# Five engines' strands interleaved by tables of knots in place of beat formulas

## Chip, cores and metric

One Trainium2 chip, one of its cores. The metric is device microseconds from start to end of one execution; lower is better. The kernel before took 2063.88 us, the median of 3 runs (2056.12 to 2064.72).

## What is computed

Two transformer blocks follow each other on 256 tokens of width 1024, all in float32. Cut to what matters:

```python
def first_block(x, mem, ...):
    x = x + token_mixer(rmsnorm(x, g_mix), ...)        # stick-breaking attention + gated delta rule
    x = x + memory_cross_attention(rmsnorm(x, g_cross), rmsnorm(mem, g_mem), ...)
    x = x + peer(rmsnorm(x, g_peer), w_pq, peer_subkeys, peer_u, peer_v)
    return rmsnorm(x, g_final)

def peer(xn, w_pq, subkeys, peer_u, peer_v):           # 8 heads, 16384 experts, top 16 each
    q = (xt @ w_pq).reshape(T, 8, 2, 128)
    s = jnp.einsum('thpd,hpnd->thpn', q, subkeys)
    top_s, top_i = lax.top_k(s, 16)
    # 256 pair sums per head, the best 16 of them, softmax gates
    act = gelu(einsum('thkd,td->thk', peer_u[expert], x)) * gate
    return einsum('thk,thkd->td', act, peer_v[expert])

def second_block(x, ...):                              # gated linear attention + spatial gating, then peer_2
```

So each block has a front of projections and attention, and then a "peer" layer in which every token picks 128 of 16384 experts.

## The kernel before, in words

The 256 tokens are two tiles of 128 (t = 0 and 1). Each of the two layers' peer parts (l = 1 and 2) handles its tiles in different ways. For tile 0 the rows of `peer_u` are gathered: 128 indirect DMAs of 128 rows by GpSimd (`rows`, through `gather`, L2328), each followed by a dot product with the normed tile. Two of three dots are done by VectorE (`experts`, L2103), every third by GpSimd (`dots`, L2351) with the sum taken by ScalarE (`experts` of the scalar program, through `act`, L1177). For tile 1 all 128 chunks of the transposed table stream through four buffers `ut_sb` (SyncE, `dense`, L592) and TensorE multiplies each (`dense`, L1013). One-hot products (`gates`, L1032) spread the gate weights. Then `values` multiplies the gates with all 128 chunks of `peer_v` (L1051, L1053, L1065), while tile 0's first 640 columns come from gathered rows (`lows`, L2328).

Before the gathers come `queries` (L977), `scores` (L992) and `select` on VectorE: per pair of heads j = 0 to 3 a strand of some 42 small pieces (`max`, `match_replace`, `max_index`, one-hot sums), of which the last writes the gather's indices `idx_sb` (L1685, signal "ix").

**What sets the order.** Each engine has one instruction stream, which it works off in order. The stream is written by a program of generators ("strands"), one for each task. A strand yields a beat (a number) before each of its pieces, and `in_turn` always advances the strand with the least beat, ties by its place in the list; a beat under the strand's last one counts as that one. The beat is a sort key and nothing else: no instruction waits for it. Waits are on semaphores and stand inside the pieces. In the kernel before the beats come from formulas: `P1(n) = 20 + 6.8 n` for the first projection, `gdn_beat`, `sel_beat`, `dense_beat`, `T_VAL` and others.

```python
        first = min(heads, key=lambda x: (x[0], x[1]))
        beat = next(first[2], None)
        ...
            first[0] = max(beat, first[0])
```

Places that the prediction touches:

- VectorE, front: `splits` (the low half of each weight chunk, `tt` at L1679, out `w_lo`) stands at `P1(n) - 4`, the pieces of `conv` of projection n at `P1(n) + 7` to `P1(n) + 9.1`. TensorE's projections (`proj`, L631 to L633) wait for `w_lo`.
- VectorE, `select(1, 0)`: pieces 35 to 40 of j = 0 (`sel_beat + 6.5 + 0.5 n`, from L1682 to L1685) stand among the cross-attention pieces of `mixer1(1)`, of which one waits for a score bank (L1956).
- ScalarE, `queries(1, 0)` piece 3 (copies a query bank to `sw_sb`, which `scores(1, 0)` piece 3 on TensorE reads) has beat 398, behind `experts(1)` pieces 16 and 19, which wait for GpSimd's dots.
- TensorE: `scores(1, 0)` piece 3 stands behind `dense(1)` pieces 0 and 1.
- Layer 2: `select(2, 0)` on VectorE stands among `mixer2(1)`, whose pieces wait for TensorE's L874; on TensorE `peer_norm(2, 0)` (transposes, L638) stands ahead of `mixer2(1)` (L874, L891).
- SyncE: the first four loads of `dense(2)` have beat 1250 and so stand behind most of the weights of `mixer2(1)` and `queries(2, ...)`, the last of which wait for TensorE.

Of the kernel before, what the change touches and what calls it, by code (L numbers as in the profile page):

```python
# [64 lines left out]


# [95 lines left out]
T_VAL = {1: (768, 2.1), 2: (1713, 2.4)}  # L162
# [65 lines left out]
def build(nc, a):  # L228
    with ExitStack() as ctx:
# [168 lines left out]
        def sync_program(e):  # L398
# [218 lines left out]
            in_turn(first(), weights(), weights2(), rows(), subkeys(), dense(1), values(1), dense(2), values(2), store())  # L617
# [3 lines left out]
        def tensor_program(e):  # L621
# [58 lines left out]
            def norm_mem():  # L680
                for t in range(2):
                    yield from transposed(ring_m, ("mem",), t, MN[:, t, :], ((28, 29), (41, 42))[t], "xs", norm_v)
# [470 lines left out]
            def sgu(t):  # L1153
# [6 lines left out]
                for g in range(4):  # L1160
# [4 lines left out]
            in_turn(norm_x(), norm_mem(), proj(), gdn(0), stick(0), row("peer", 1, ring_c, ROW, 124), mixer1(0), memory(), stick(1),  # L1165
                    peer_norm(1, 0), gdn(1), queries(1, 0), scores(1, 0), mixer1(1), experts(1, 0), peer_norm(1, 1), queries(1, 1), scores(1, 1),
                    dense(1), experts(1, 1), gates(1, 1), gates(1, 0), values(1), row("final", 1, ring_c, ROW, T_VAL[1][0] + 20),
                    row("ln", 1, ring_c, LNR, 970), norm_2(), keys(), proj2(), gla(0), sgu(0), gla(1), sgu(1),
                    row("peer", 2, ring_c, ROW, 1161), mixer2(0), mixer2(1), peer_norm(2, 0), queries(2, 0), scores(2, 0), experts(2, 0),
                    peer_norm(2, 1), queries(2, 1), scores(2, 1), dense(2), experts(2, 1), gates(2, 1), gates(2, 0), values(2),  # L1170
                    row("final", 2, ring_c, ROW, T_VAL[2][0] + 20))


        def scalar_program(e):
# [488 lines left out]
            def sgu(t):  # L1663
# [4 lines left out]
            in_turn(norm_x(), splits(), norm_mem(), proj(), silus(), betas(), gdn(0), stick(0), row("peer", 1, ROW, 126), mixer1(0), memory_hi(),  # L1668
                    memory(), stick(1), gdn(1), peer_norm(1, 0), mixer1(1), queries(1, 0), softmax(1, 0), experts(1), peer_norm(1, 1),
                    queries(1, 1), softmax(1, 1), dense(1), gates(1, 1), gates(1, 0), values(1), row("final", 1, ROW, T_VAL[1][0] + 21),  # L1670
                    row("ln", 1, LNR, 971), final(1, 0), final(1, 1), norm_2(), keys(), proj2(), gla(0), sgu(0), gla(1), sgu(1),
                    row("peer", 2, ROW, 1162), peer_norm(2, 0), queries(2, 0), softmax(2, 0), experts(2), peer_norm(2, 1),
                    queries(2, 1), softmax(2, 1), dense(2), gates(2, 1), gates(2, 0), values(2), row("final", 2, ROW, T_VAL[2][0] + 21),
                    final(2, 0), final(2, 1))

        def vector_program(e):
# [573 lines left out]
            def sgu(t):  # L2250
# [27 lines left out]
                else:  # L2278
# [3 lines left out]
            in_turn(norm_x(0), norm_x(1), splits(), norm_mem(), conv(), betas(), gdn(0), stick(0), mixer1(0), memory_lo(), stick(1), gdn(1), peer_norm(1, 0),  # L2282
                    experts(1), weights(1), select(1, 0), mixer1(1), peer_norm(1, 1), select(1, 1), gates(1, 1), dense(1), gates(1, 0), lows(1),
                    values(1), sums_out(1, 0), sums_out(1, 1), final(1, 0), final(1, 1), norm_2(), gla(0), sgu(0), gla(1), sgu(1),
                    mixer2(0), mixer2(1), peer_norm(2, 0), experts(2), weights(2), select(2, 0), peer_norm(2, 1), select(2, 1), gates(2, 1), dense(2), gates(2, 0),
                    lows(2), values(2), sums_out(2, 0), sums_out(2, 1), final(2, 0), final(2, 1))


        def gpsimd_program(e):
# [190 lines left out]
```

## Time and profile before

| | us |
|---|---|
| median of 3 runs | 2063.88 |
| lowest and highest run | 2056.12, 2064.72 |
| span of the profiled execution | 2058.1 |
| TensorE busy in it | 1900.5 |
| VectorE busy | 1377.4 |
| ScalarE busy | 901.4 |
| GpSimd busy | 773.3 |
| mean granted TensorE clock | 0.981 of full speed |

The profiled execution has no time of its own beside its span, which lies inside the spread of the three runs and 5.8 us under their median. Times are counted from its first instruction. Busy time of TensorE counts pipelined matmuls as one stretch, so it holds some waiting too. A stretch of the kernel is named by its start and end in microseconds.

### The profile page before, as it was taken

The numbers are of one execution on the slowest core, as the hardware profiler recorded it, in microseconds if no ns is written. First come the engines' busy times: TensorE is split into PE (matmuls) and PEld (weight loads), VectorE is DVE, ScalarE is ACT, GpSimd is POOL, SyncE is SP. The second block draws the span as 40 slices with busy tenths as digits, with TensorE's granted clock in tenths as the row PEclk, the third lists the DMA queues.
The fourth block names the chain that finished last, engine by engine and source line by source line (L and its number), as shares of the span: only waits on it lengthen the run. The fifth ranks groups of instructions, "written<-read, shape, count | busy, mean of one in ns | idle before, by whom it ended". The sixth has DMA issues, their size and how long they took to land. (4 is left out here: it accounts for less than half of the span.)

```text
span 2058.1 us, 32947 instructions
## 1 busy us (share of the span) xinstructions
PE 1900.5 (92%) x12722; PEld 1667.2 (81%) x12722; DVE 1377.4 (67%) x2723; ACT 901.4 (44%) x1945; POOL 773.3 (38%) x626
## 2 busy tenths in 40 slices
PE   6999999987888989999999999898898899899998
PEld 6999988887888989776666889898897899677774
DVE  6643431379889948588785244168798888688884
ACT  5545443123335737544442454103233668544442
POOL 0000000058676634344441000037677555444441
PEclk9999999998999999999999999999999999999999
DMA  6433453899999988999997334679999998899996
GB/s 231 162 121 114 161 198 132 347 357 342 384 372 409 384 319 290 330 379 401 397 394 271 133 134 144 245 313 378 408 393 404 356 325 286 296 378 388 391 389 253
DMA packets 154298, 622.89 MB, mean 303 GB/s; under 512 B 19207, under 2 KB 22919, under 8 KB 138782
## 3 DMA queue, kind: packets, MB, share of 16 engines
q1 hardware_dynamic: 96798, 402.65, 51.9%
q0 software_dynamic: 57344, 218.14, 27.8%
q8 instruction: 101, 1.65, 0.3%
q14 instruction: 55, 0.45, 0.1%
HBM read 619.66 MB, written 1.05 MB: 302 GB/s over the span
## 5 line engine op out<-in xcount | busy, mean ns | idle before, releaser
L1013 PE MATMUL bank<-nt_sb,ut_sb 128*128 128x128 f32 x4096 | 505.3, 280 | 47.0 <-DMA ut_sb<-in_ut_dram 42.5
L1013 PEld LDWEIGHTS bank<-nt_sb,ut_sb 128*128 128x128 f32 x4096 | 483.9, 196 | 58.5 <-DMA ut_sb<-in_ut_dram 42.8
L2328 POOL DMA_INDIRECT big_sb<-in_u_dram,idx_sb x256 | 254.1, 993 | 243.6 <-ACT big_sb L1177 115.2
L1177 ACT ACTIVATE big_sb<-bank 128x512 f32<-128x512 f32 (+11 forms) x282 | 131.4, 479 | 330.9 <-PE bank L1013 108.1
L2292 POOL TENSOR_TENSOR sm_sb<-sm_sb,vec_sb 128x1 f32<-128x1 f32 (+2 forms) x24 | 19.4, 812 | 637.6 <-DVE sm_sb L1682 632.0
L2103 DVE CUSTOM_DVE_ANT_0 big_sb<-big_sb,bank_n 128x1024 f32<-128x1024 f32 x170 | 205.4, 1210 | 52.1 <-DMA big_sb<-in_u_dram,idx_sb 47.9
L2351 POOL TENSOR_TENSOR big_sb<-big_sb,nt_sb 128x1024 f32<-128x1024 f32 x86 | 204.3, 2377 | 10.7 <-DMA big_sb<-in_u_dram,idx_sb 7.7
L631 PE MATMUL bank<-n_hi,w_hi 128*128 128x256 f32 x608 | 180.4, 297 | 13.6 <-DVE w_lo L1679 13.4
L1177 ACT ACTIVATE big_sb<-big_sb 128x1024 f32<-128x1024 f32 (+2 forms) x132 | 116.5, 884 | 152.9 <-POOL big_sb L2351 139.5
L1065 PE MATMUL bank_n<-v_hi,g_hi 128*128 128x384 f32 x240 | 177.4, 739 | 0.0
L2328 POOL DMA_INDIRECT cst_sb<-in_vl_dram,idx_sb x102 | 120.9, 1185 | 144.6 <-DVE x_sb L1685 141.5
L632 PE MATMUL bank<-n_hi,w_lo 128*128 128x256 f32 x608 | 175.1, 288 | 0.0
L633 PE MATMUL bank<-n_lo,w_hi 128*128 128x256 f32 x608 | 175.0, 288 | 0.0
L1679 DVE TENSOR_TENSOR g_lo<-big_sb,g_hi 128x256 fp32r<-128x256 f32 x240 | 105.1, 438 | 104.2 <-ACT g_hi L1177 100.6
L2328 POOL DMA_INDIRECT spare_sb<-in_vl_dram,idx_sb x102 | 108.6, 1065 | 136.0 <-DVE x_sb L1685 125.9
L1679 DVE TENSOR_TENSOR w_lo<-big_sb,w_hi 128x2048 fp32r<-128x2048 f32 x46 | 105.2, 2289 | 69.2 <-ACT w_hi L1177 69.2
L1177 ACT ACTIVATE v_hi<-nt_sb 128x512 fp32r<-128x512 f32 x120 | 75.8, 632 | 139.9 <-issue 93.4
L1051 PE MATMUL bank<-nt_sb,big_sb 128*128 128x512 f32 x260 | 132.9, 592 | 3.7 <-DMA nt_sb<-in_v_dram 3.7
L631 PEld LDWEIGHTS bank<-n_hi,w_hi 128*128 128x128 f32 x608 | 119.8, 197 | 19.3 <-issue 16.7
L977 PE MATMUL bank<-nt_sb,big_sb 128*128 128x128 f32 x1024 | 121.2, 278 | 1.5 <-DMA big_sb<-in_wall_dram 0.7
L977 PEld LDWEIGHTS bank<-nt_sb,big_sb 128*128 128x128 f32 x1024 | 119.0, 195 | 2.3 <-issue 2.2
L632 PEld LDWEIGHTS bank<-n_hi,w_lo 128*128 128x128 f32 x608 | 120.0, 197 | 0.5 <-issue 0.5
(270 smaller groups left out, 4069.0 us busy)
## 6 DMA issues: line engine op xcount, KB each, us to landing
ut_sb<-in_ut_dram SPq DMA_DIRECT2D x256, 512.0 KB
big_sb<-in_wall_dram SPq DMA_DIRECT2D x119, 1024.0 KB, 9.9
nt_sb<-in_v_dram SPq DMA_DIRECT2D x130, 512.0 KB
sw_sb<-in_v_dram SPq DMA_DIRECT2D x84, 512.0 KB
ab_sb<-in_v_dram SPq DMA_DIRECT2D x42, 512.0 KB
big_sb<-in_u_dram,idx_sb POOLq DMA_INDIRECT x256
cst_sb<-in_vl_dram,idx_sb POOLq DMA_INDIRECT x102
spare_sb<-in_vl_dram,idx_sb POOLq DMA_INDIRECT x102
```

The costliest lines, as they stand in the source:

```text
L631: e.matmul(out, lh(k), rh(k), start=k == 0, stop=False)
L632: e.matmul(out, ll(k), rh(k), start=False, stop=False)
L633: i = e.matmul(out, lh(k), rl(k), start=False, stop=k == 7)
L977: i = e.matmul(hs(bk, 2 * (h % 2) + c), w[:, k * 256 + c * 128:k * 256 + (c + 1) * 128], TN[t][:, k, :], start=k == 0, stop=k == 7)
L1013: i = e.matmul(hs(bk, c % 4), UT[:, c % DR, k * 128:(k + 1) * 128], TN[1][:, k, :], start=k == 0, stop=k == 7)
L1051: i = e.matmul(total[1][0], GM[:, 1, c, :], VSL[vslot(s)][:, 0:RAW_COLS], start=s == 0, stop=s == LAST[1])
L1065: i = e.matmul(total[1][1] if t else total[0], x[:, w, :], y[:, b, (0 if t else FD - RAW_COLS):], start=part == 0 and s == 0, stop=False)
L1177: return e.activation(out, in_, func, bias=bias, scale=scale, **kw)
L1679: return e.tensor_tensor(out, x, y, op)
L2103: e.tensor_tensor_reduce(g, g, NP[:, :], 1.0, 0.0, ALU.mult, ALU.add, H[:, k:k + 1]).then_inc(*dot_v.up("dot", l, k))
L2328: return e.indirect_dma_start(out, None, table, bass.IndirectOffsetOnAxis(ap=IDX[:, k:k + 1], axis=0))
L2351: e.tensor_tensor(UB[k % UR], UB[k % UR], N[:, 0, :], ALU.mult).then_inc(*dot_g.up("dot", l, k))
```

## The change

A wrapper `paced` drops the beats that a strand yields and gives it others, from a table of knots (piece number, beat), with straight lines between the knots. All 173 strands of the five engines are wrapped. The pieces, what is in them, their waits, and their order within a strand are as before; only how the strands of one engine are interleaved differs. Merging the new beats by the rule of `in_turn` and comparing with the order before, the least number of pieces that have to be taken out and put elsewhere is 666 of 2275 on VectorE, 242 of 1368 on ScalarE, 182 of 1778 on TensorE, 77 of 623 on GpSimd and 20 of 657 on SyncE.

```diff
+def paced(strand, knots):
+    at = 0
+    for n, _ in enumerate(strand):
+        if at + 1 < len(knots) and n >= knots[at + 1][0]:
+            at += 1
+        (k, b), (m, c) = knots[at], knots[min(at + 1, len(knots) - 1)]
+        yield b + (c - b) * (n - k) / (m - k) if m > k else b
+PACE = {
+    "sync": {
...
+        ('dense', 2): ((0, 1224), (1, 1233.4), (2, 1256.1), (3, 1263.2), (4, 1300.2), (5, 1326.6), (12, 1340.2), (14, 1351.9), (47, 1437.7),
...
+    "scalar": {
...
+        ('queries', 1, 0): ((0, 370.4), (1, 408.7), (2, 409.2), (3, 442.4),),
+        ('experts', 1): ((0, 370.4), (1, 402.8), (3, 404.1), (4, 416.3), (6, 417.4), (7, 423.4), (10, 425.3), (11, 433.9), (15, 435), (18, 437.7),
+            (19, 449), (21, 450.1), (23, 457.6), (26, 461.1), (28, 461.1), (29, 465.6), (31, 465.6), (32, 480.2), (34, 480.7), (35, 487.3),
...
+    "vector": {
...
+        ('splits',): ((0, 9.4), (1, 9.5), (2, 11.8), (3, 15.8), (4, 18), (5, 32.6), (6, 37.8), (8, 53.4), (9, 59.2), (11, 67.2), (12, 82.2), (13, 87),
...
+        ('conv',): ((0, 27.6), (6, 29.7), (7, 34.8), (20, 43.9), (21, 48.6), (41, 58.9),),
...
+        ('experts', 1): ((0, 391.53), (1, 402.89), (2, 403.56), (3, 404.74), (4, 406.76), (5, 407.52), (6, 416.62), (7, 417.8), (8, 424.47),
...
+        ('select', 1, 0): ((0, 378.85), (1, 379.32), (4, 379.93), (12, 382.03), (16, 382.85), (17, 383.25), (18, 383.35), (22, 384.4), (24, 384.83),
+            (25, 384.92), (29, 386.01), (32, 386.59), (35, 387.4), (37, 387.68), (40, 391.34), (41, 399.7), (42, 412.54), (43, 416.01), (45, 416.42),
...
+        ('mixer1', 1): ((0, 339.9), (1, 340.8), (4, 353.1), (6, 369.6), (7, 369.6), (10, 372), (11, 378.3), (12, 398.9), (14, 406.8), (15, 412),
...
+        ('select', 2, 0): ((0, 1269.6), (1, 1285.2), (37, 1294.1), (39, 1299.8), (40, 1301), (63, 1306.4), (64, 1308.1), (75, 1310.6), (76, 1312.1),
...
+        ('mixer2', 1): ((0, 1266.91), (1, 1292.74), (3, 1297.79), (4, 1306.7), (5, 1314.96),),
...
+    "tensor": {
...
+        ('scores', 1, 0): ((0, 377.9), (1, 414.6), (2, 438.1), (3, 448.2),),
+        ('dense', 1): ((0, 449.2), (3, 455), (4, 460.8), (9, 470.5), (10, 476.4), (14, 485.7), (16, 497.4), (18, 502.2), (19, 511.9), (24, 521.6),
...
+        ('mixer2', 1): ((0, 1264.9), (5, 1271.2), (6, 1288.6), (15, 1297.3), (19, 1310.9),),
+        ('peer_norm', 2, 0): ((0, 1268.7), (1, 1269.2),),
+        ('queries', 2, 0): ((0, 1272.1), (3, 1284.7), (4, 1314.5), (5, 1318.4), (6, 1339.9), (7, 1345.7),),
...
+        ('values', 2): ((0, 1696), (481, 1947.3), (489, 1953), (496, 1966.2),),
...
-            in_turn(first(), weights(), weights2(), rows(), subkeys(), dense(1), values(1), dense(2), values(2), store())
+            pace = PACE["sync"]
+            in_turn(paced(first(), pace[('first',)]), paced(weights(), pace[('weights',)]), paced(weights2(), pace[('weights2',)]),
...
```

The other four engines' calls of `in_turn` are changed in the same way.

## Rows read from the trace of the kernel before

**Rows 1.** The page: busy time, then the clock in 40 slices.

```profile
PE 1900.5 (92%) x12722; PEld 1667.2 (81%) x12722; DVE 1377.4 (67%) x2723; ACT 901.4 (44%) x1945; POOL 773.3 (38%) x626
...
PEclk9999999998999999999999999999999999999999
```

**Rows 2.** Busy time by stretch: length, then each engine, clock, DMA share, GB/s.

```profile
0.00:38.00 38.00, 24.89 (x182) 23.44 (x183) 22.63 (x46) 19.96 (x32) 2.58 (x8) 1.00 0.71 282
38.00:385.00 347.00, 329.44 (x2498) 312.22 (x2497) 144.22 (x216) 158.61 (x238) 8.39 (x6) 0.99 0.45 161
385.00:845.00 460.00, 409.65 (x3406) 399.28 (x3406) 359.49 (x839) 208.05 (x532) 263.82 (x201) 0.97 0.93 352
845.00:1108.00 263.00, 257.76 (x968) 177.67 (x969) 207.51 (x348) 114.15 (x245) 111.18 (x100) 0.99 0.99 383
1108.00:1325.00 217.00, 203.75 (x1318) 177.19 (x1316) 74.59 (x100) 82.88 (x133) 5.85 (x9) 0.98 0.46 165
1325.00:1776.00 451.00, 401.51 (x3343) 390.10 (x3343) 356.03 (x823) 201.56 (x518) 273.92 (x201) 0.98 0.91 344
1776.00:2031.00 255.00, 255.00 (x967) 179.00 (x968) 207.66 (x344) 114.10 (x244) 106.49 (x100) 0.99 0.98 380
2031.00:2058.00 27.00, 18.54 (x47) 8.32 (x45) 5.32 (x11) 2.06 (x6) 1.11 (x2) 0.93 0.57 210
```

**Rows 3.** The page's costliest groups: streamed chunks on TensorE, dots on VectorE.

```profile
L1013 PE MATMUL bank<-nt_sb,ut_sb 128*128 128x128 f32 x4096 | 505.3, 280 | 47.0 <-DMA ut_sb<-in_ut_dram 42.5
...
L2103 DVE CUSTOM_DVE_ANT_0 big_sb<-big_sb,bank_n 128x1024 f32<-128x1024 f32 x170 | 205.4, 1210 | 52.1 <-DMA big_sb<-in_u_dram,idx_sb 47.9
```

**Rows 4.** Timeline of TensorE and of VectorE in the first projection.

```profile
41.47 0.36 PE L631 MATMUL bank<-n_hi,w_hi 128*128 128x256 f32 x1 [1.84 <-DVE w_lo L1679]
...
50.27 0.35 PE L631 MATMUL bank<-n_hi,w_hi 128*128 128x256 f32 x1 [1.96 <-DVE w_lo L1679]
...
39.04 2.28 DVE L1679 TENSOR_TENSOR w_lo<-big_sb,w_hi 128x2048 fp32r<-128x2048 f32 x1
```

**Rows 5.** Timeline of VectorE, then GpSimd, before the first gather of layer 1.

```profile
402.89 0.27 DVE L1682 TENSOR_SCALAR su_sb<-su_sb 128x32 uint32<-128x32 uint32 x2
411.97 0.69 DVE L1956 TENSOR_REDUCE sm_sb<-bank 128x2 f32<-128x512 f32 x1 [8.81 <-PE bank L921]
...
418.25 0.19 DVE L1685 SCALAR_TENSOR_TENSOR idx_sb<-ef_sb 128x32 uint32<-128x32 f32 x1
...
418.74 1.15 POOL L2328 DMA_INDIRECT big_sb<-in_u_dram,idx_sb  x1 [31.64 <-DVE idx_sb L1685]
```

**Rows 6.** Timeline of TensorE, then of ScalarE, at 480 us; then one stretch.

```profile
481.59 2.05 PE L992 MATMUL bank<-sub_sb,sw_sb 128*128 128x128 f32 x8 [9.65 <-DVE su_sb L2051]
...
479.86 1.06 ACT L1177 ACTIVATE big_sb<-big_sb 128x1024 f32<-128x1024 f32 x1 [4.84 <-POOL big_sb L2351]
...
480.91 0.58 ACT L1177 ACTIVATE sw_sb<-bank 128x512 f32<-128x512 f32 x1
...
482.00:488.00 6.00, 6.00 (x32) 6.00 (x32) 5.90 (x17) 2.11 (x3) 5.21 (x5) 0.55 0.87 285
```

**Rows 7.** Timeline before the first gather of layer 2: TensorE, VectorE, GpSimd.

```profile
1323.01 1.72 PE L638 MATMUL bank<-cst_sb,nt_sb 128*128 128x128 f32 x8 [3.29 <-DVE nt_sb L1685]
...
1344.32 0.69 DVE L1679 TENSOR_TENSOR nt_sb<-bank,big_sb 128x512 f32<-128x512 f32 x1 [4.39 <-PE bank L874]
...
1351.46 0.69 DVE L1679 TENSOR_TENSOR nt_sb<-bank,big_sb 128x512 f32<-128x512 f32 x1 [4.59 <-PE bank L874]
...
1365.25 1.02 POOL L2328 DMA_INDIRECT big_sb<-in_u_dram,idx_sb  x1 [43.17 <-DVE sv_sb L2090]
```

**Rows 8.** GpSimd's dots by line (min/median/max ns), and VectorE beside one of them.

```profile
L2351 POOL TENSOR_TENSOR big_sb<-big_sb,nt_sb x86: 2343/2364/2643, 429.4 to 1686.5; 128x1024 f32<-128x1024 f32 x86
...
437.85 3.02 DVE L1679 TENSOR_TENSOR sw_sb<-sv_sb 128x240 f32<-128x240 f32 x2
...
1346.09 0.51 DVE L1679 TENSOR_TENSOR sw_sb<-sv_sb 128x240 f32<-128x240 f32 x2
```

More of the change, by code:

```diff
@@ L615, in store @@
                                     X[:, t, h * 512:(h + 1) * 512]).then_inc(*out_in[t].up(h))
-            in_turn(first(), weights(), weights2(), rows(), subkeys(), dense(1), values(1), dense(2), values(2), store())
+            pace = PACE["sync"]
+            in_turn(paced(first(), pace[('first',)]), paced(weights(), pace[('weights',)]), paced(weights2(), pace[('weights2',)]),
+                    paced(rows(), pace[('rows',)]), paced(subkeys(), pace[('subkeys',)]), paced(dense(1), pace[('dense', 1)]),
+                    paced(values(1), pace[('values', 1)]), paced(dense(2), pace[('dense', 2)]), paced(values(2), pace[('values', 2)]),
+                    paced(store(), pace[('store',)]))
             for t in range(2):
@@ L1163, in sgu @@
                 i.then_inc(*sgu_p.up(t))
[L1165 to L1171, printed above, removed]
+            pace = PACE["tensor"]
@@ L1666, in sgu @@
                 act(SW[:, 512:1024], SW[:, 0:512], ACT.Square, accum_out=small(1, "sss", t)).then_inc(*sgu_a.up(t))
[L1668 to L1674, printed above, removed]
+            pace = PACE["scalar"]
@@ L2280, in sgu @@
                 tt(Y2[t][:, 512:1024], ring_c.place(("sgu", t))[:, :], SUT[t], ALU.mult).then_inc(*sgu_v.up(t, "yb"))
[L2282 to L2286, printed above, removed]
+            pace = PACE["vector"]
@@ L2374, in sgu @@
                 root(small(1, "sr", t), small(1, "sm", t), 1).then_inc(*sgu_g.up(t))
-            in_turn(norms(), gdn(0), gdn(1), rows(1), dots(1), lows(1), sgu(0), gla(0), gla(1), sgu(1), rows(2), dots(2), lows(2))
+            pace = PACE["gpsimd"]
+            in_turn(paced(norms(), pace[('norms',)]), paced(gdn(0), pace[('gdn', 0)]), paced(gdn(1), pace[('gdn', 1)]),
+                    paced(rows(1), pace[('rows', 1)]), paced(dots(1), pace[('dots', 1)]), paced(lows(1), pace[('lows', 1)]),
+                    paced(sgu(0), pace[('sgu', 0)]), paced(gla(0), pace[('gla', 0)]), paced(gla(1), pace[('gla', 1)]), paced(sgu(1), pace[('sgu', 1)]),
+                    paced(rows(2), pace[('rows', 2)]), paced(dots(2), pace[('dots', 2)]), paced(lows(2), pace[('lows', 2)]))
         programs = {"sync": sync_program, "gpsimd": gpsimd_program, "scalar": scalar_program, "vector": vector_program, "tensor": tensor_program}
```

279 lines of the change are left out of this document (added), and 105 rows, old and new, of the table PACE.

## The prediction

> **What bounds the kernel now.** The page comes first: TensorE is busy for 1900.5 us of the span of 2058.1, no other engine for more than 67% [rows 1]. So TensorE stands for 158 us, and the clock line shows full speed nearly throughout; its mean of 0.981 is worth at most 39 us more. A change of order can win nothing but such losses. The table of stretches says where they lie [rows 2]. In the two stretches of `values` (845 to 1108, 1776 to 2031) TensorE loses 5.2 and 0 us: there the matmuls themselves are the time, and no order shortens them. The losses are in the front (38 to 385: 17.6), in the peer stage of layer 1 (385 to 845: 50.4), in the front of layer 2 (1108 to 1325: 13.2) and in its peer stage (1325 to 1776: 49.5). Adding the clock (one less its share, times the length) makes these 21, 64, 18 and 59 us, 161 in all. The start (13.1) and the end (8.5) are chains in which each step needs the one before.
>
> In the peer stages the DMA share is 0.93 and 0.91 and VectorE is busy for 359 and 356 us of 460 and 451 [rows 2]. The costliest groups show what the two wait for: TensorE's streamed chunks for their loads, 42.5 us in all, and VectorE's 170 dots for their gathered rows, 47.9 us [rows 3]. So a peer stage is DMA traffic first, vector work second and matmuls third, all three near full, and it lasts as long as the gathers are late plus what TensorE can't do meanwhile.
>
> **The change part by part.** No operation, wait, buffer or byte is added or taken away; each engine's work stays what it is. What changes is who stands behind whom. I read the order from the beats and look at what stood still at those places.
>
> Front, VectorE. The low half of a weight chunk has its beat ahead of the convolution pieces that it followed: chunk 3 at 32.6 against 34.8 for the first of its convolution. TensorE waits 1.84 and 1.96 us for such halves [rows 4], and the half at 39.04 could have run in VectorE's time before 36.1. That is 3.8 us. Of the 17 that the front loses beside these (17.6 idle and 3.5 clock, less 3.8) I take 10, since many strands of attention wait on each other across four engines there, which an order helps only in part. Sum 14, bounds 0 and 21. What the moved halves push back is convolution, which feeds the attention strand; its cover is the row of projections, at 6 us a pair.
>
> Peer stage 1, gathers. The first gather leaves at 418.74, when its indices are there. VectorE stood for 8.81 us before them, at a piece of the cross attention that waits for a score bank, with the last six selection pieces queued behind it [rows 5]. In the new tables selection pieces 35 to 40 have beats 387.4 to 391.3 and that attention piece 398.9, so they no longer wait: 8.8 us, and about 1 of attention work between them, 10 in all. The attention piece loses nothing, for its bank comes at 412 anyhow. All 128 gathers shift with the first. I count 8 of the 10, as the stretch after the last gather is bounded by TensorE.
>
> Peer stage 1, TensorE. At 481.59 a score group ends a stop of 9.65 us, and the next six microseconds run at a granted clock of 0.55, so 2.7 more [rows 6]. The profile names VectorE, but the indices' work had long gone on; what ended a moment before is ScalarE's copy to `sw_sb` at 480.91, which stood behind a sum of a GpSimd dot that had itself waited 4.84. The new ScalarE table has that copy at 442.4, ahead of `experts` piece 19 at 449, and the scores ahead of `dense` pieces 0 and 1. That takes 12 us away. Sum of the stage 20; bounds 0, if the chunks' loads turn out to be what ends each wait, and 44 (12, 10 and half of the 42.5 for chunks).
>
> Front 2. Five up-projection pieces of tile 1 now come ahead of the transposes that wait 3.29 us [rows 7], at some 0.9 us each; 3.3, and a third of the other 14, so 8; bounds 0 and 18. The first chunks' loads on SyncE move ahead of weights that wait, which costs these weights their issue time alone.
>
> Peer stage 2. The selection stood for 4.39 and 4.59 us at pieces of `mixer2(1)` before the gather at 1365.25 [rows 7]; the new table runs selection pieces 1 to 37 in one go. That is 9, and the order of copies, sums and scores is mended as in layer 1, for which I take the same 12; sum 21, bounds 0 and 44. Values and end: 3 of the 5.2, bounds 0 and 8.
>
> Sum: 14 + 20 + 8 + 21 + 3 = 66 us. The profiled execution has its span of 2058.1, some 6 under the median; the saving is the same against either. **Forecast: 2063.9 - 66 = 1998 us.** A measurement can tell about 0.5% (10 us) from no change.
>
> **What speaks against it.** GpSimd's 86 dots last 2.36 us each, and VectorE's two short additions that met one at 437.85 took 3.02 us where the same two take 0.51 alone [rows 8]. So a dot that runs holds such operations of VectorE up. The new tables have the pieces there at 0.2 to 0.4 us apart and leave no room for it. The Trainium skill has this as a rule ("SBUF — State Buffer", section "Who interferes with whom"): a VectorE instruction with two SBUF inputs and a GpSimd one that reads SBUF exclude each other for a whole instruction. The trace agrees, with the 3.02. That page gives no price for it here.
>
> **Rivals.**
>
> 1. The tables are kept to the end. Their last piece of `values(2)` has beat 1966.2, and the tables' steps in `values(2)` are (1947.3 - 1696) / 120 = 2.09 us, where TensorE was busy for 255 us of 255 [rows 2], about 122 such steps, so the knots are written in microseconds. If all came as they say, the end would be near 1975 in the trace and 1980 as a run: 84 saved of the 183 that TensorE loses (161, 13 and 8.5). For it: no single step is out of reach. Against: it needs each stage to win at or past the middle of my bounds. With some luck in the DMA traffic it could go to 1965.
> 2. Half is kept. VectorE is held up by GpSimd's dots: 86 dots, each holding one operation for half its length, are 101 us of VectorE's time. It has 101 and 95 us free in the peer stages [rows 2], so a late index or gate product comes back as a stop of TensorE. Then the stages give 10 each in place of 20 and 21, and the front half: 30 to 40 saved, 2030.
> 3. Slower. Dots stand ahead of selection pieces: `experts(1)` pieces 2 to 5 have beats 403.6 to 407.5, ahead of selection piece 42 at 412.5. A dot whose row hasn't landed stops VectorE with the next indices and gates behind it, and then GpSimd's gathers, which wait for both. Before, 170 dots waited 47.9 us, 0.28 each [rows 3]. Each 0.1 us more is 17 us of VectorE in stages where it is four fifths full. If all of it lands on the path, it eats the 66 at 0.4 us more a dot, and at 0.6 more the run is 102 - 66 = 36 us longer, 2100. For it: gathers compete with chunks at a DMA share above 0.9. Against: the gathers start earlier than now, ahead of the stream of chunks.
> 4. Nothing changes: the stops only move, since each engine waits for the DMA traffic. Then 2064, give or take 10. Against: TensorE stands at 41, 50 and 481 us for work of VectorE and ScalarE, not for a load [rows 4, 6].
>
> **How the numbers follow.** My forecast (1985 to 2018) has 0.42, the tables kept (1965 to 1985) 0.24, half kept (2018 to 2053) 0.21, no change 0.06, slower 0.07. Faster is the first three, 0.87; same 0.06; slower 0.07. The range runs from 1967 to 2043: it cuts a little off the best case, the last third of the half case, and the last two cases, some 0.2 in all.
>
> **What would show it.** The first gather of layer 1 issued at some 385 to 400 in place of 418.7, and of layer 2 at 1300 to 1325; no idle row of VectorE over 5 us between the first selection piece and the indices. No stop of TensorE near 10 us at its last score group of tile 0, and the copy to `sw_sb` right after the queries. First `values` matmuls near 812 and 1720, and their stretches as long as before (some 280 us each to the last matmul). TensorE busy about the same, its idle time down from 158 to near 100. It is wrong if the dots' waits (47.9) grow past 100 us, or if the 42.5 us for chunks take up what the other stops give back.

## The result, and the profile after

The changed kernel took 2008.22 us, the median of 4 runs (2000.48 to 2013.67), against 2062.74 us (2056.12 to 2064.72) for the kernel before on the same chips: a ratio of 0.974, 95% interval 0.9714 to 0.9766. That is 54 us less, where 66 were forecast; 2008 lies inside the range and inside the likeliest case (1985 to 2018). The sum came out well. The experiments below show that its parts did so less. The profiled execution is the fastest of the four (2000.48), 7.7 us under their median, so the two profiles differ by some 5 us more than the runs do.

The page of the changed kernel, against [rows 1]: busy time, then the granted clock.

```profile
span 1998.7 us, 32943 instructions
...
PE 1889.2 (95%) x12722; PEld 1652.4 (83%) x12722; DVE 1353.6 (68%) x2723; ACT 891.2 (45%) x1941; POOL 794.4 (40%) x626
...
PEclk9999999999999999999999999999999999899999
```

The span fell by 59.4 us. TensorE's idle time (span less busy) fell from 157.6 to 109.5, that is 48.1, and its busy time by 11.3 with the same 12722 matmuls. The second part goes with the clock: its mean rose from 0.981 to 0.989, so what is lost to it fell from 39 to 22 us of the span. The other three runs of the changed kernel have 0.983 to 0.986, and 25 other runs of the kernel before have 0.974 to 0.982, so the gain in clock is real, though this profile shows it at its best. Each of the two stops of some 10 us shown here goes with a stretch at the lower of the clock's two levels (granted 0.55 in [rows 6], 0.51 below), so a removed stop can pay twice.

The table of stretches, cut where TensorE starts a new kind of work (columns as in [rows 2]).

```profile
0.00:38.00 38.00, 25.31 (x173) 23.50 (x174) 21.26 (x39) 17.50 (x29) 3.37 (x8) 1.00 0.71 282
38.00:367.50 329.50, 326.64 (x2507) 310.36 (x2507) 144.19 (x223) 157.54 (x239) 7.47 (x7) 0.99 0.47 171
367.50:816.50 449.00, 405.44 (x3407) 394.43 (x3407) 357.62 (x841) 206.45 (x532) 267.75 (x202) 0.98 0.95 359
816.50:1100.20 283.70, 280.17 (x1025) 188.19 (x1026) 209.66 (x357) 118.13 (x254) 116.09 (x102) 0.99 0.97 373
1100.20:1286.10 185.90, 184.43 (x1309) 170.53 (x1309) 69.56 (x89) 77.47 (x124) 4.78 (x7) 0.99 0.50 182
1286.10:1716.30 430.20, 392.85 (x3301) 379.50 (x3299) 345.61 (x828) 198.50 (x517) 280.94 (x206) 0.99 0.93 359
```

| TensorE reaches | before | after | earlier by | this stretch gave | forecast |
|---|---|---|---|---|---|
| first query matmul, layer 1 | 385.5 | 367.5 | 18.0 | 18.0 | 14 |
| first `values` matmul, layer 1 | 845.4 | 816.5 | 28.9 | 10.9 | 20 |
| last `values` matmul, layer 1 | 1130.0 | 1100.2 | 29.8 | 0.9 | |
| first query matmul, layer 2 | 1325.5 | 1286.1 | 39.4 | 9.6 | 8 |
| first `values` matmul, layer 2 | 1776.0 | 1716.3 | 59.7 | 20.3 | 21 |
| end | 2058.1 | 1998.7 | 59.4 | -0.3 | 3, with layer 1's |

Six pieces of `mixer2(1)`, some 5.4 us of matmuls, now stand ahead of layer 2's first query and not behind it, so the two rows of layer 2 are better read as 15 and 15. In the front TensorE is idle for 2.9 of 329.5 us: what [rows 4] showed is gone. In the two peer stages it is still idle for 44 and 37 us.

The costliest groups of the page, against [rows 3] (the last one is GpSimd's dots).

```profile
L1373 PE MATMUL bank<-nt_sb,ut_sb 128*128 128x128 f32 x4096 | 495.3, 278 | 47.8 <-DMA ut_sb<-in_ut_dram 40.5
...
L2494 DVE CUSTOM_DVE_ANT_0 big_sb<-big_sb,bank_n 128x1024 f32<-128x1024 f32 x170 | 202.6, 1213 | 60.1 <-DMA big_sb<-in_u_dram,idx_sb 57.0
...
L2757 POOL TENSOR_TENSOR big_sb<-big_sb,nt_sb 128x1024 f32<-128x1024 f32 x86 | 207.2, 2411 | 45.9 <-DMA big_sb<-in_u_dram,idx_sb 41.6
```

The waits for chunks stay as they were (40.5 against 42.5). VectorE's dots wait a little more for their rows (57.0 against 47.9), and GpSimd's dots wait for rows now, 41.6 us against 7.7. I put that down to the tables, which place them sooner behind their gathers; no run isolates it.

Timelines of the changed kernel around the start of layer 1's gathers (VectorE, then GpSimd) and at the end of tile 1's cross attention (VectorE, then TensorE), against [rows 5, 6]; the last row is a stretch as above.

```profile
389.39 0.19 DVE L2076 SCALAR_TENSOR_TENSOR idx_sb<-ef_sb 128x32 uint32<-128x32 f32 x1
394.91 1.22 DVE L2494 CUSTOM_DVE_ANT_0 big_sb<-big_sb,bank_n 128x1024 f32<-128x1024 f32 x1 [5.33 <-DMA big_sb<-in_u_dram,idx_sb]
...
389.88 1.15 POOL L2734 DMA_INDIRECT big_sb<-in_u_dram,idx_sb  x1 [20.15 <-DVE idx_sb L2076]
...
445.67 2.83 DVE L2076 SCALAR_TENSOR_TENSOR nt_sb<-x_sb,sm_sb,row_sb 128x512 f32<-128x512 f32 x1 [1.44 <-POOL sm_sb L2698]
...
450.60 0.73 DVE L2076 SCALAR_TENSOR_TENSOR nt_sb<-x_sb,sm_sb,row_sb 128x512 f32<-128x512 f32 x1
...
448.64 1.09 PE L998 MATMUL bank<-cst_sb,nt_sb 128*128 128x128 f32 x4 [8.06 <-DVE nt_sb L2076]
451.47 1.09 PE L998 MATMUL bank<-cst_sb,nt_sb 128*128 128x128 f32 x4 [1.75 <-DVE nt_sb L2076]
...
445.80:456.20 10.40, 5.81 (x27) 5.47 (x28) 10.33 (x43) 4.17 (x9) 6.51 (x5) 0.51 0.78 266
```

The first gather leaves 22.4 us after TensorE's first query in place of 33.3, and its indices had no wait in front of them. But the stop of 9.65 us, which stood ahead of the last score group at 481.59, has a successor: TensorE stands for 8.06 and 1.75 us at the transposes of tile 1's norm, and from 445.8 on, within this stop, its clock is at the lower level for 10.4 us (granted 0.51, that is 1.2 GHz). The first half of VectorE's norm product took 2.83 us there, beside a GpSimd dot of 2.35 us that began at 445.59; the second half, with no dot beside it, took 0.73. Between the two halves stood nine selection pieces. The kernel before had a stop at these transposes too:

```profile
463.47 1.88 PE L638 MATMUL bank<-cst_sb,nt_sb 128*128 128x128 f32 x8 [4.87 <-DVE nt_sb L1685]
```

So the norm and the last score group together cost 4.87 and 9.65 us of standing before, 14.5, and cost 9.8 now.

### The profile page after: what moved, and what is told of

It reads as the page before. It is cut to its first block and busy times, and to the rows that moved or that the text cites. A ratio compares the mean times of both kernels' runs of the same rounds, so it can differ in the third digit from the quotient of the medians.

```text
span 1998.7 us, 32943 instructions
## 1 busy us (share of the span) xinstructions
PE 1889.2 (95%) x12722; PEld 1652.4 (83%) x12722; DVE 1353.6 (68%) x2723; ACT 891.2 (45%) x1941; POOL 794.4 (40%) x626
## 5 line engine op out<-in xcount | busy, mean ns | idle before, releaser
L1373 PE MATMUL bank<-nt_sb,ut_sb 128*128 128x128 f32 x4096 | 495.3, 278 | 47.8 <-DMA ut_sb<-in_ut_dram 40.5
L1373 PEld LDWEIGHTS bank<-nt_sb,ut_sb 128*128 128x128 f32 x4096 | 474.7, 193 | 59.5 <-DMA ut_sb<-in_ut_dram 35.3
L1552 ACT ACTIVATE big_sb<-bank 128x512 f32<-128x512 f32 (+12 forms) x282 | 130.1, 477 | 232.0 <-PE bank L1373 56.9
L2757 POOL TENSOR_TENSOR big_sb<-big_sb,nt_sb 128x1024 f32<-128x1024 f32 x86 | 207.2, 2411 | 45.9 <-DMA big_sb<-in_u_dram,idx_sb 41.6
L2734 POOL DMA_INDIRECT spare_sb<-in_vl_dram,idx_sb x102 | 119.7, 1174 | 135.9 <-DVE x_sb L2076 105.3
L2734 POOL DMA_INDIRECT cst_sb<-in_vl_dram,idx_sb x102 | 127.4, 1249 | 111.2 <-DVE x_sb L2076 101.6
L1552 ACT ACTIVATE w_hi<-big_sb 128x2048 fp32r<-128x2048 f32 x46 | 87.8, 1909 | 73.2 <-PE bank L993 66.8
L993 PEld LDWEIGHTS bank<-n_lo,w_hi 128*128 128x128 f32 x608 | 118.9, 196 | 0.0
```

Of the source, the lines that this page charges most:

```text
L993: i = e.matmul(out, lh(k), rl(k), start=False, stop=k == 7)
L1373: i = e.matmul(hs(bk, c % 4), UT[:, c % DR, k * 128:(k + 1) * 128], TN[1][:, k, :], start=k == 0, stop=k == 7)
L1552: return e.activation(out, in_, func, bias=bias, scale=scale, **kw)
L2734: return e.indirect_dma_start(out, None, table, bass.IndirectOffsetOnAxis(ap=IDX[:, k:k + 1], axis=0))
L2757: e.tensor_tensor(UB[k % UR], UB[k % UR], N[:, 0, :], ALU.mult).then_inc(*dot_g.up("dot", l, k))
```

## Experiments

Each ratio is against runs of the kernel before that were taken beside the run. A difference between two of these runs is uncertain by 6 to 9 us unless said otherwise, and one profile of a stage differs from another of the same order by several us: the layer 1 peer stage took 449.0, 449.9, 449.6 and 457.8 us in four kernels whose order there is the new one (one has a slightly changed tail). In four kernels whose order there is the old one, with no piece of the stage moved, it took 459.9, 455.7, 459.1 and 455.7.

### Single moves in the kernel before

**b_copy**: the move behind my 12 us for TensorE's stop.

```diff
-FIRST_TURNED = (322, 347, 366, 398)
-FIRST_SCORE = (325, 350, 379.2, 400)
+FIRST_TURNED = (322, 347, 366, 380.5)
+FIRST_SCORE = (325, 350, 379.2, 383.9)
```

> The kernel before, with one thing changed: ScalarE's fourth query copy of tile 0 (layer 1) stands right behind its second cross-attention square instead of behind two sums of GpSimd dots, and TensorE's fourth score group stands ahead of the first dense chunks. My theory (the term of 12 us): TensorE's stop of 9.65 us at 481.6 goes and the stretch at half clock behind it too, so the first values matmul comes 8 to 12 us earlier than 845.4 and the run is 8 to 12 us shorter (about 2053). Rival (the stage is bounded by its loads and gathers): the stop goes but the chunks wait for their loads instead, the first values matmul moves by 0 to 3 us, and the run is the same within 0.2 per cent.

Measured 2056.6 us, ratio 0.9984 (0.9968 to 0.9999): 3 us less, at most 7. TensorE's timeline in it:

```profile
464.49 1.84 PE L638 MATMUL bank<-cst_sb,nt_sb 128*128 128x128 f32 x8 [4.85 <-DVE nt_sb L1685]
471.41 2.08 PE L992 MATMUL bank<-sub_sb,sw_sb 128*128 128x128 f32 x8 [5.08 <-DVE su_sb L2023]
473.28 6.95 PE L1013 MATMUL bank<-nt_sb,ut_sb 128*128 128x128 f32 x54
```

ScalarE's copy is now there at 462.1, and the score group still waits, 5.08 us, until VectorE's search through the third pair's scores (L2023) gives the bank back. In the kernel before, that search ended at 470.34, ahead of the stop, which began at 471.94 behind 32 matmuls of the first dense chunks. So it cost nothing there. The move put the score group ahead of those matmuls, and thereby ahead of the search, and the first dense chunks start at 473.3 where they had started at 466.1. The copy alone, with the group left behind the chunks, was not run. In this profile the stage is 6.5 us shorter (453.4 against 459.9); over ten runs 3 us are left.

**b_sel**: the move behind my 8 to 10 us for the gathers' start.

```diff
-                    yield 253.8 + s + 2.5 * n
+                    yield 349.05 if t == 1 and n == 0 else 253.8 + s + 2.5 * n
```

> The kernel before, with one thing changed: on VectorE the cross-attention piece of tile 1 that waits for a score bank stands behind the last six selection pieces of the first pair of heads. My theory (the term of 8 to 10 us): the first gather leaves near 409 in place of 418.7, the 128 gathers end some 9 us earlier than 733, and the run is 8 us shorter (about 2055). Rival (TensorE and its chunks bound the stage, not the gathers): the first gather is as early, but the last gather ends at most 4 us earlier or the first values matmul moves by less than 3 us, and the run is the same within 0.2 per cent.

Measured 2061.8 us, ratio 1.0004 (0.9992 to 1.0015): no change, and this interval is narrow enough to rule out more than 2 us of gain. GpSimd's timeline, first and last gathers of layer 1:

```profile
411.63 1.15 POOL L2328 DMA_INDIRECT big_sb<-in_u_dram,idx_sb  x1 [21.71 <-DVE idx_sb L1685]
...
730.94 1.01 POOL L2328 DMA_INDIRECT big_sb<-in_u_dram,idx_sb  x1 [1.71 <-ACT big_sb L1177]
732.26 0.94 POOL L2328 DMA_INDIRECT big_sb<-in_u_dram,idx_sb  x1 [0.30 <-issue]
```

The first query of this profile comes at 389.3, 3.8 us later than in the kernel before. Nothing had been moved up to there (b_both, with the same edit, has 386.6), so times are best counted from it. The gathers start 22.4 us after it, as in the changed kernel, in place of 33.3. In the kernel before the last gather left at 732.29, 346.8 us after the first query; here it leaves 343.0 after it, and in b_both 343.2. Four kernels with the old start of the gathers (b_copy, b_split, b_split2 and h_front) have 339.8 to 346.1, so the lead of 10.9 us is not to be found at the last gather: from first to last they take 321.6 us in place of 314.5. There are eight row buffers, and in this stretch GpSimd waits 53 us for a dot's sum on ScalarE and 14 us for a VectorE dot to give a buffer back (57 and 3 before). I read this as the pace of the dots setting the end, and not the start of the gathers; it holds for this order, as a_undo and h_c1331 will show.

**b_both**, the two together.

> The two moves of the runs b_copy and b_sel together. My theory (independent terms): the gains add, 16 to 20 us, the first values matmul near 827, the run about 2045. Rival (one shared bound, DMA traffic): 0 to 5 us. Between: if only one of them is worth anything, this run equals that one.

Measured 2056.78 us, ratio 0.9983 (0.9968 to 0.9999): b_copy's result, nothing on top. Of the 20 us of my two terms 3 are there. The sum is excluded; 3 us lies in the rival's 0 to 5, and it is what the better of the two moves gives alone.

**b_split**: the move behind my 3.8 us in the front.

```diff
-                    yield from split_one(("in", n), P1(n) - 4)
+                    yield from split_one(("in", n), P1(n) - 7)
```

> The kernel before, with one thing changed: VectorE's low half of each weight chunk of the first projection has a beat 3 lower, so that it stands ahead of the convolution pieces of the chunk before. My theory (3.8 us in the front): TensorE's waits of 1.84 and 1.96 us at 41.5 and 50.3 go, its last projection matmul comes near 191 in place of 194.9, and the rest of the front shifts with it: 3 to 4 us, 2060. Rival (the attention strand bounds the front, not the projection): the projection ends earlier but the first query matmul stays at 385 within 1 us, and the run doesn't change.

Measured 2075.01 us, ratio 1.008 (1.0057 to 1.0103): 16 us longer, a sign that neither theory had. The first query matmul comes at 403.7. Timelines of ScalarE, VectorE and TensorE in it:

```profile
42.41 0.72 ACT L1177 ACTIVATE big_sb<-sw_sb 128x256 f32<-128x256 f32 x2 [4.77 <-DVE sw_sb L1685]
43.04 1.90 ACT L1177 ACTIVATE w_hi<-big_sb 128x2048 fp32r<-128x2048 f32 x1
...
44.97 2.29 DVE L1679 TENSOR_TENSOR w_lo<-big_sb,w_hi 128x2048 fp32r<-128x2048 f32 x1 [2.60 <-ACT w_hi L1177]
...
77.71 1.44 PE L733 MATMUL bank<-vec_sb,big_sb 128*128 128x1 f32 x6 [6.79 <-ACT big_sb L1177]
```

ScalarE's gate waits for VectorE's convolution, its high half stands behind that gate, VectorE's low half waits for the high half, and the next convolution pieces now stand behind the low half. Each chunk goes once around that ring. The delta-rule strand, which needs the convolutions, starts at 77.7 in place of 69.6.

**b_split2** moves ScalarE's high halves too.

```diff
-                    yield from split_one(("in", n), 8 + 6 * n if n < 2 else P1(n) - 6 if n > 5 else P1(n) - 9)
+                    yield from split_one(("in", n), 8 + 6 * n if n < 2 else P1(n) - 9 if n > 5 else P1(n) - 12)
```

> As b_split (the kernel before with VectorE's low halves of the first projection's chunks 3 beats earlier), and ScalarE's high halves 3 beats earlier too, so that they stand ahead of the gates (silus) that wait for VectorE's convolution. Theory: b_split lost 18 us in the front because the two engines then waited for each other in turn (low half on high half, high half behind a gate, the gate on the convolution, that behind the low half). Then this run gives the 18 us back and the 3.8 us on top: first query matmul at 380 to 386, the run at 2057 to 2061. Rival: the convolution is simply too late behind the low halves whatever ScalarE does: then the front stays at 395 or more and the run at 2070 or more.

Measured 2071.7 us, ratio 1.0056 (1.0033 to 1.0079): still 12 us longer than before, first query at 399.9. The ring explains a part at most. ScalarE's third high half of a chunk now stands ahead of the squares of the memory's norm and waits for a free weight slot:

```profile
26.49 1.92 ACT L1177 ACTIVATE w_hi<-big_sb 128x2048 fp32r<-128x2048 f32 x1 [10.36 <-PE bank L633]
```

It comes at 26.49, where it had come at 24.28 with all four squares ahead of it. In the changed kernel two of those four squares stand ahead of that half, and the first gate behind the two halves after it. Moved alone, these pieces cost more than they save; which neighbours of theirs the rest of the 12 us hangs on stays open.

### One thing altered in the changed kernel

**a_undo** puts VectorE's waiting piece back ahead of the last six selection pieces.

```diff
-        ('mixer1', 1): ((0, 339.9), (1, 340.8), (4, 353.1), (6, 369.6), (7, 369.6), (10, 372), (11, 378.3), (12, 398.9), (14, 406.8), (15, 412),
+        ('mixer1', 1): ((0, 339.9), (1, 340.8), (4, 353.1), (6, 369.6), (7, 369.6), (10, 372), (11, 378.3), (12, 387.3), (14, 406.8), (15, 412),
```

> The changed kernel with one knot put back in the old order: on VectorE the cross-attention piece that waits for a score bank stands ahead of the last six selection pieces of the first pair again (layer 1). The first gather should leave some 8 us later than 389.9. Theory of single waits: the run is 6 to 9 us longer, 2014 to 2017. Theory of a shared bound: the stage's gathers take less time from the first to the last (314 in place of 322 us) and the run is 0 to 3 us longer.

Measured 2011.87 us, ratio 0.9765 (0.9742 to 0.9788), against 0.974 for the change: 5 us longer, where 0 is inside the uncertainty. VectorE, GpSimd and TensorE in it:

```profile
394.06 0.69 DVE L2347 TENSOR_REDUCE sm_sb<-bank 128x2 f32<-128x512 f32 x1 [8.82 <-PE bank L1281]
406.10 1.22 DVE L2494 CUSTOM_DVE_ANT_0 big_sb<-big_sb,bank_n 128x1024 f32<-128x1024 f32 x1 [6.84 <-DMA big_sb<-in_u_dram,idx_sb]
...
399.55 1.15 POOL L2734 DMA_INDIRECT big_sb<-in_u_dram,idx_sb  x1 [29.70 <-DVE idx_sb L2076]
...
418.82 1.41 PE L1352 MATMUL bank<-ab_sb,sw_sb 128*128 128x128 f32 x5 [8.59 <-ACT sw_sb L1552]
```

The gathers leave 9.7 us later, the first dot waits for its row ahead of the cross attention, and TensorE stops for 8.59 us at the second score group, a stop that neither kernel has. In this profile, unlike in b_sel, the last gather moves with the first: it leaves at 722.94 where the changed kernel has 710.85, 355.4 us after the first query, while the four kernels that keep the new order there have 342.6 to 348.1. The first `values` matmul comes at 827.5 in place of 816.5. So in this order the early start seems to be worth something, by another way than mine (in the old order no dot stood there, and TensorE did not stop); the runs alone, 5 us, do not show it beyond their noise.

**a_tail** takes the stop at 448.64: tile 1's last addition and norm ahead of selection and dots on VectorE, the root ahead of a dot on GpSimd, ScalarE and TensorE to match.

```diff
 vector:
-            (16, 432.5), (17, 441),),
-        ('peer_norm', 1, 1): ((0, 440.7), (1, 443.4), (2, 443.8), (3, 447),),
+            (16, 432.5), (17, 432.5),),
+        ('peer_norm', 1, 1): ((0, 434.4), (1, 434.41), (2, 437.4), (3, 437.4),),
 gpsimd:
-        ('norms',): ((0, 0), (3, 8.1), (4, 26.7), (5, 178.6), (6, 313.4), (7, 338.5), (8, 441.4), (9, 1053), (10, 1074.1), (11, 1077.1), (12, 1090.8),
+        ('norms',): ((0, 0), (3, 8.1), (4, 26.7), (5, 178.6), (6, 313.4), (7, 338.5), (8, 433.7), (9, 1053), (10, 1074.1), (11, 1077.1), (12, 1090.8),
 scalar:
-        ('peer_norm', 1, 1): ((0, 430.5), (2, 447.6), (3, 448.2),),
+        ('peer_norm', 1, 1): ((0, 430.5), (1, 434.4), (2, 442.5), (3, 442.5),),
 tensor:
-        ('scores', 1, 0): ((0, 377.9), (1, 414.6), (2, 438.1), (3, 448.2),),
-        ('peer_norm', 1, 1): ((0, 446.8), (1, 447.3),),
+        ('scores', 1, 0): ((0, 377.9), (1, 414.6), (2, 438.1), (3, 443.3),),
+        ('peer_norm', 1, 1): ((0, 443.1), (1, 443.2),),
```

> The changed kernel with five table rows of the end of tile 1's cross attention (layer 1) altered: on VectorE its last addition and the two halves of the norm before the peer layer come ahead of selection and dots, on GpSimd the root ahead of a dot, and ScalarE and TensorE follow. It aims at the stop of 8.06 and 1.75 us that TensorE has there at 440 to 451, with 5 us at half clock. Theory of single waits: the first dense chunk starts at about 445 in place of 454, the first values matmul 7 to 10 us earlier than 816, the run near 2000 against 2008. Theory of a shared bound (after the two runs b_sel and b_both): the stop goes, and the gathers, dots and chunks take the time back by the stage's end; 0 to 3 us, 2005 to 2008.

Measured 2007.63 us, ratio 0.9744 (0.9721 to 0.9766): the same as the change. TensorE's timeline:

```profile
444.03 1.75 PE L998 MATMUL bank<-cst_sb,nt_sb 128*128 128x128 f32 x8 [2.24 <-DVE nt_sb L2076]
450.21 2.08 PE L1352 MATMUL bank<-sub_sb,sw_sb 128*128 128x128 f32 x8 [4.43 <-issue]
452.08 1.27 PE L1373 MATMUL bank<-nt_sb,ut_sb 128*128 128x128 f32 x5
```

The norm's stop shrank from 9.81 to 2.24 us, and 4.43 us stand now at the score group. The profile names no releaser for it, but VectorE's search through the third pair, which gives the bank back, ends its last piece at 450.16. By that it is the wait that b_copy met. The edit shortened the stops and did not remove them, so it doesn't test what a removed one would give.

**a_halfut** leaves out half of the columns of the streamed chunks' loads; TensorE multiplies what lay there, so the peer layers' products for tile 1 are changed.

```diff
-                    e.dma_start(UT[:, c % DR, :], a[f"ut{l}"][4 * dense_place(l, c // 4) + c % 4]).then_inc(*ut_in[c % DR].up(l, c))
+                    w = D if c < DR else D // 2
+                    e.dma_start(UT[:, c % DR, 0:w], a[f"ut{l}"][4 * dense_place(l, c // 4) + c % 4][:, 0:w]).then_inc(*ut_in[c % DR].up(l, c))
```

> The changed kernel, in which all but the first four loads of the streamed table of each layer bring only half of a chunk's columns (256 KB instead of 512); TensorE's matmuls are the same and use what lay there, so this part of the computation is changed. It takes 63 MB of 623 away, all in the peer stages. If DMA traffic is the shared bound: the waits for chunks (40.5 us) and for gathered rows (57.0 and 41.6) fall by more than half, the peer stages get 15 us or more shorter each, the run comes to 1965 to 1980. If VectorE's queue of dots and selection is the bound: the DMA share falls from 0.95 to about 0.8, the stages get 0 to 5 us shorter each, 1998 to 2008.

Measured 1978.22 us, ratio 0.9596 (0.9575 to 0.9618): 30 us less than the change. Its groups, then its two peer stages:

```profile
L1374 PE MATMUL bank<-nt_sb,ut_sb 128*128 128x128 f32 x4096 | 491.1, 278 | 21.7 <-DMA ut_sb<-in_ut_dram 15.2
...
L2495 DVE CUSTOM_DVE_ANT_0 big_sb<-big_sb,bank_n 128x1024 f32<-128x1024 f32 x170 | 202.0, 1211 | 35.1 <-DMA big_sb<-in_u_dram,idx_sb 29.2
...
L2758 POOL TENSOR_TENSOR big_sb<-big_sb,nt_sb 128x1024 f32<-128x1024 f32 x86 | 205.1, 2389 | 18.5 <-DMA big_sb<-in_u_dram,idx_sb 17.1
...
367.50:813.00 445.50, 409.64 (x3409) 400.21 (x3407) 364.84 (x841) 205.94 (x531) 268.32 (x202) 0.97 0.82 289
1286.00:1702.00 416.00, 390.28 (x3320) 381.26 (x3318) 351.48 (x829) 199.75 (x519) 280.63 (x206) 0.99 0.84 293
```

65 MB less traffic, a tenth of the whole and a fifth of what the two peer stages move, and the waits for chunks and for rows about halve, as the traffic theory said; the run came to its upper end. In this profile the stage of layer 2 is 14 us shorter than the change's and that of layer 1 only 4, both under the 15 each that the theory named. The profiled run is the slowest of its five (1988.5), so how the 30 us divide stays uncertain.

**a_dots** cuts GpSimd's products from 1024 to 128 columns, which leaves most of every third dot out.

```diff
-                    e.tensor_tensor(UB[k % UR], UB[k % UR], N[:, 0, :], ALU.mult).then_inc(*dot_g.up("dot", l, k))
+                    e.tensor_tensor(UB[k % UR][:, 0:128], UB[k % UR][:, 0:128], N[:, 0, 0:128], ALU.mult).then_inc(*dot_g.up("dot", l, k))
```

> The changed kernel with GpSimd's 86 products cut from 1024 to 128 columns, so that a dot of 2.41 us becomes one of some 0.3 to 0.5 us and most of those dots' products are left out; the sums on ScalarE keep their length. Theory that GpSimd's dots hold VectorE up (my second rival): VectorE's stretched operations (55 us in all by the trace of the changed kernel) go, the peer stages get 10 us or more shorter each, 1985 or less. If this hold-up is hidden behind the traffic: 0 to 5 us in all, 2003 to 2008.

Measured 1999.95 us, ratio 0.9721 (0.9693 to 0.9749): 4 us less than the change, with nothing at all inside the uncertainty, and 15 us not.

```profile
PE 1886.2 (95%) x12722; PEld 1649.8 (83%) x12722; DVE 1302.0 (65%) x2723; ACT 889.8 (45%) x1941; POOL 628.1 (32%) x626
...
L2494 DVE CUSTOM_DVE_ANT_0 big_sb<-big_sb,bank_n 128x1024 f32<-128x1024 f32 x170 | 203.0, 1214 | 71.2 <-DMA big_sb<-in_u_dram,idx_sb 69.8
```

VectorE's busy time falls by 51.6 us (by 55 and 59 against the profiles of a_undo and a_tail), the stretching that my second rival was about, and so it is real. The Trainium skill's rule ("SBUF — State Buffer", section "Who interferes with whom") agrees with it, and with the norm product of 2.83 us above. But VectorE's waits for rows rise from 57.0 to 69.8, and the run gains 4 us with 8 uncertain. So most of that hold-up is hidden. Whether all of it is, this run does not show: in its profile, the fastest of its four, the peer stage of layer 1 takes 438.8 us (449.0 to 457.8 in the four with whole products) and that of layer 2 427.5 (430.2 in the changed kernel).

### The new order up to a point, the old one behind it

In these every engine takes the pieces that it had begun before a time T of the changed kernel's trace in the new order, and the rest in the old one.

```diff
+def listed(order, *strands):
+    for s in strands:
+        next(s, None)
+    for n, count in order:
+        for _ in range(count):
+            next(strands[n], None)
...
-            in_turn(paced(norm_x(0), pace[('norm_x', 0)]), paced(norm_x(1), pace[('norm_x', 1)]), paced(splits(), pace[('splits',)]),
+            listed(ORDER["vector"], paced(norm_x(0), pace[('norm_x', 0)]), paced(norm_x(1), pace[('norm_x', 1)]), paced(splits(), pace[('splits',)]),
```

**h_front** (T = 367.5), **h_l1** (900) and **h_c1331** (1331):

> All five engines follow the new order for the pieces that the changed kernel had begun before 367.5 us (its first query matmul of layer 1), and the old order for all that is left. If what the front of layer 1 gains is kept to the end: the first query matmul at some 367 to 370 in place of 385.5, the first values matmul near 828, the run 16 to 18 us shorter than before (2044 against 2061). If a peer stage takes it back (its loads and gathers don't start earlier): 0 to 8 us.

> As h_front, but the new order holds for the pieces begun before 900 us (so for all of layer 1's peer stage), and the old one from there on. If the stages' gains add: the first values matmul of layer 1 near 816, and 27 to 31 us less than before (2032), half of what the whole change gives; layer 2's part is then the rest. If layer 1's part depends on how the orders match rather than on the stage: under 20 or over 40 us.

> As h_l1, but the new order holds for the pieces begun before 1331 us: all of layer 2's front and the start of its peer stage, up to the first gather and the last piece of tile 1's second mixer on VectorE. By my steps (8 us in the front, 9 us from the earlier start of the gathers): the first gather at some 31 us after the first query matmul in place of 40, and 17 to 18 us less than h_l1's 2034.6, so 2017; the rest to the whole change's 2008 is then the later order's. By the theory that the gathers' pace and the traffic set the stage and not its start (as b_sel and a_halfut say of it): the first gather is as early, but only the front's 8 to 10 us are kept, 2025, and the later order brings the other 16.

| new order up to | median | ratio (95%) | less than before | this part gave | my terms |
|---|---|---|---|---|---|
| 367.5, front of layer 1 | 2040.22 | 0.9899 (0.9878 to 0.9921) | 20.8 | 20.8 | 14 |
| 900, peer stage of layer 1 | 2034.58 | 0.9873 (0.9851 to 0.9895) | 26.2 | 5.4 | 20 |
| 1331, front 2 and first gather | 2016.00 | 0.9778 (0.9744 to 0.9813) | 45.8 | 19.6 | 8 + 9 |
| the end | 2008.22 | 0.9740 (0.9714 to 0.9766) | 53.6 | 7.8 | 12 + 3 |

("Less than before" is the ratio times 2062; each part is uncertain by 6 to 9 us.) GpSimd's first gather of layer 2 in h_l1 and in h_c1331:

```profile
1337.86 1.02 POOL L2810 DMA_INDIRECT big_sb<-in_u_dram,idx_sb  x1 [43.16 <-DVE sv_sb L2557]
```

```profile
1324.48 1.02 POOL L2809 DMA_INDIRECT big_sb<-in_u_dram,idx_sb  x1 [36.19 <-DVE su_sb L2489]
```

These come 40.1 and 30.8 us after the first query. The front's gain is kept to the end, and more of it than forecast. Layer 1's peer stage gave a quarter of its term; its 5.4 is no more than the uncertainty of the difference. Layer 2's start gave what my steps said, not what b_sel had led me to expect in its place; the later order of its stage gave less than its term.

The two traces show where the 19.6 arises. From the first `values` matmul of layer 1 to the first query of layer 2 it is 479.8 us in h_l1 and 468.1 in h_c1331, and from there to the first `values` matmul of layer 2 450.1 and 440.5. The lead of h_c1331 is whole at the last gather: its first gather leaves 13.4 us earlier than that of h_l1, its last 13.95 (1638.05 and 1652.00), and its `values` begin 13.7 earlier. So in layer 2, unlike in b_sel, the last gather moves with the first.

## Why the prediction was right or wrong

**What bounds the kernel.** Right: the gain came out of TensorE's standing and clock, and the two `values` stretches kept their length (284.5 and 283.7; 275.1 and 275.4). "DMA traffic first" is borne out by a_halfut: 30 us for a tenth of the bytes, more than any single order step in a peer stage. (Those bytes are a fifth of what the peer stages move.)

**The front, 14 us: right in size, wrong in its step.** The marks give 18.0, h_front 20.8. But the step I priced, low halves ahead of convolutions for 3.8, costs 16 us when done alone. The sentence that failed is "What the moved halves push back is convolution ...; its cover is the row of projections": that work had no cover in this order, and moving ScalarE's halves along with it gave back some 5 of the 16, with 7 uncertain (b_split2). What the tables did was mend the front as a whole; I counted a lump of 10 for that, and the gain can only be told for the whole.

**Peer stage 1, 20 us: too much by some 10 to 15.** The marks give 10.9, the runs 5.4; between the means of the four profiles of each order it is 6.0. Both of its terms failed. The 12 us: "What ended a moment before is ScalarE's copy" was true, but the move that went with it, the scores "ahead of `dense` pieces 0 and 1", put the group ahead of a search on VectorE that it had not had to wait for: 5.08 us in b_copy, 4.43 in a_tail, and in the changed kernel 9.81 at the norm just ahead, where 4.87 had been. I priced the end of one wait and not the next one at the new place. The 8 us: "All 128 gathers shift with the first; I count 8 of the 10" is what b_sel disproves for the old order: the start moved, the last gather didn't. Nor does the changed kernel have its last gather much earlier in the stage (343.4 us after the first query, against 346.8), though a_undo's comes later still.

**Front 2 and peer stage 2, 8 and 21 us: right within what can be told.** 9.6 and 20.3 by the marks, 27.4 together by the runs. Here an early gather start and the front's order did come out at the end: 19.6 for 17. No run separates those two, so how much of the 19.6 is the gathers' and how much the front's stays open. By the marks of h_l1 and h_c1331 11.7 arise ahead of the first query, 17 with the 5.4 us of matmuls that moved there, so the front may well be under-sized at 8 and the gathers' 9 too large. That the last gather followed the first is seen; that the earlier start alone did it is not shown. The 12 us copied from layer 1 had no better ground there than here; 7.8 came.

**Values and end, 3 us:** 0.6.

**The clock** is a term that I left too small. I had 3.5 in the front and 2.7 at one stop; its loss fell by 17 us of the span, more than half of which stands nowhere in the sum.

**The rivals.** Half kept (2030) by VectorE's hold-up: the hold-up exists, and taking most of it away gives 4 us with 8 uncertain (a_dots), not the 30 or so that it was to cost. Slower by dots that wait: 57.0 us on VectorE, far from the 100 named. With GpSimd's dots, which I had left out of that sign, it is 98.6 against 55.6, and the run is faster all the same. Nothing changes: excluded by the result. Tables kept (1980): they fell behind by steps; dense chunk 0 has beat 449.2 and came at 454.1, `values(2)` has 1696 and came at 1716.3. The first of these has the stop at 448.64 ahead of it.

**The signs given.** First gathers at 389.88 and 1316.94: as said. `values` at 816.5 and 1716.3 for "812 and 1720", idle time 109.5 for "near 100". No idle row over 5 us ahead of the indices: so it is. TensorE busy about the same: 11 less. No stop near 10 us at the score group: so it is, but one of 8.06 and 1.75 us stands one step ahead of it.

So 54 for 66 is in part luck: by the runs the parts gave 7 more, 15 less, 3 more and 7 less than their terms, and only the sum of these, -12, shows in the result. Of the four only the 15 is well clear of the uncertainty of such a difference; the 7 more in the front is just clear of its own (4 us).

## What to carry to other kernels

Before a stop is priced at its length, ask which wait comes second, and at the new place of the moved piece rather than the old: take the last one away on paper and look when the next would be met. In a stage that cycles through a few buffers an earlier start can be worth nothing (b_sel) or be kept to the last transfer (layer 2), so look at the last one before counting it. And where several engines feed each other in a ring, price an order as a whole or not at all: one piece moved alone lost 16 us here, where the whole new order of that stretch gained 21.

## What the runs showed of the hardware that was not expected

TensorE's 12722 matmuls took 11.3 us less busy time with no change to them (1889.2; a_tail and a_undo, whose orders are nearly the new one, have 1894.1 and 1895.4 against 1900.5 before). Around the stop at 448.64 the granted clock is 0.51 for 10.4 us, from 445.8, while TensorE stands and after it. An order with fewer stops is paid in clock as well, in this pair of profiles 11 us for 48 us of idle time. And 51.6 us of VectorE's busy time went when GpSimd's products were cut to an eighth. They were waiting inside VectorE's own operations, which a busy share doesn't show, and they cost the run 4 us, with 8 uncertain.
